# Dots that read normalised rows from PSUM, a weighted sum in one bank, and a fifth slot for v rows

## The reference, cut to what matters

```python
y, k_new, v_new, s_new = token_mixer(rmsnorm(h, norm1), ...)   # 8 attention heads and 4 recurrent heads
h = h + y
h = h + peer(rmsnorm(h, norm2), peer_w_q, peer_sub_keys, peer_u, peer_v)
out = rmsnorm(h, final_norm)

def peer(xn, ...):                       # per block of 128 tokens
    s = einsum('thcd,hcnd->thcn', qh, sub_keys)          # 8 heads, 2 halves, 128 keys
    ... top 16 of each half, of their 256 sums the top 16: 128 experts eidx a token
    act = gelu(einsum('td,thkd->thk', xb, u_tab[eidx]))  # u_tab: 16384 x 1024
    return einsum('thk,thkd->td', g * act, v_tab[eidx])  # v_tab: 16384 x 1024
```

## Time and profile before

| | |
|---|---|
| time, median of 3 runs | 4234.32 us (4230.32 to 4242.23) |
| span of the profiled execution, its own time | 4312.9 us |
| PE, DVE, POOL, ACT busy | 68%, 62%, 61%, 24% |
| moved by DMA | 1387.82 MB, mean 322 GB/s |
| gathers | 1152 of u, 1152 of v |

### The profile page before, as it was taken

One profiled execution on the slowest core, in us unless ns is written; L12 is line 12 of the kernel. 1 busy time (PEld: TensorE's weight loads), 2 busy tenths in 40 slices (PEclk: granted clock), 3 DMA queues, 4 the chain that ended last, 5 costly groups with the idle time before them and its releaser, 6 DMA issues. The chain is left out here.

```text
span 4312.9 us, 52328 instructions
## 1 busy us (share of the span) xinstructions
PE 2945.6 (68%) x18028; PEld 1552.0 (36%) x18028; DVE 2685.8 (62%) x7647; ACT 1054.1 (24%) x2841; POOL 2646.5 (61%) x2365
## 2 busy tenths in 40 slices
PE   7889997876577648774877487748784565333365
PEld 6745553533253325432443244325442231000011
DVE  2456667756875777567756876687658656644400
ACT  3312212222232222222222222222222211111121
POOL 1102434666776676577666765775567767777765
PEclk9999998777577758685778577857786666555556
DMA  7535898999999999898989998998898999999998
GB/s 202 179 127 184 283 334 287 334 367 347 331 344 366 332 332 335 312 357 323 333 312 364 342 335 308 364 339 319 307 358 309 377 361 359 329 371 364 364 368 316
DMA packets 568774, 1387.82 MB, mean 322 GB/s; under 512 B 57384, under 2 KB 252384, under 8 KB 568512
## 3 DMA queue, kind: packets, MB, share of 16 engines
q0 software_dynamic: 335024, 1215.35, 76.6%
q1 hardware_dynamic: 221264, 159.49, 11.9%
q10 hardware_dynamic: 12224, 9.63, 0.8%
HBM read 1353.19 MB, written 30.95 MB: 321 GB/s over the span
## 5 line engine op out<-in xcount | busy, mean ns | idle before, releaser
L1805 DVE CUSTOM_DVE_ANT_0 d_ub<-d_ub,d_xn 128x1024 f32<-128x1024 f32 x1152 | 1404.7, 1222 | 950.8 <-DMA d_ub<-in_peer_u_dram,d_eid 855.2
L1611 POOL DMA_INDIRECT d_ub<-in_peer_u_dram,d_eid x1152 | 1292.5, 1122 | 807.6 <-issue 313.5
L1628 POOL DMA_INDIRECT d_vb<-in_peer_v_dram,d_eidT x1088 | 1263.4, 1161 | 708.0 <-PE d_pY L1656 383.7
L1656 PE MATMUL d_pY<-d_vb,d_dg 128*32 128x256 f32 x8704 | 938.9, 522 | 1070.1 <-DMA d_vb<-in_peer_v_dram,d_eidT 949.0
L1656 PEld LDWEIGHTS d_pY<-d_vb,d_dg 128*32 128x32 f32 x8704 | 237.6, 127 | 1668.8 <-issue 1492.0
L1696 ACT ACTIVATE d_dg<-c_late_sb,d_wgtT 128x32 f32<-128x32 f32 x1152 | 342.4, 315 | 1399.9 <-PE d_pY L1656 1149.5
L680 PE MATMUL d_pY<-d_wq,d_vb 128*128 128x512 f32 (+3 forms) x1536 | 473.0, 461 | 14.2 <-DMA d_vb<-in_w_in_dram 7.7
L680 PEld LDWEIGHTS d_pY<-d_wq,d_vb 128*128 128x128 f32 x1536 | 269.4, 198 | 182.5 <-issue 115.5
L816 PE MATMUL d_pS<-t_shared 32*128 32x512 f32 (+3 forms) x384 | 194.9, 707 | 52.6 <-DMA t_shared<-scratch_kT 43.2
L827 PE MATMUL d_pS<-t_mdg,t_E 128*128 128x128 f32 x1152 | 219.0, 361 | 13.2 <-DVE t_mdg L1036 11.2
L827 PEld LDWEIGHTS d_pS<-t_mdg,t_E 128*128 128x128 f32 x1152 | 199.6, 266 | 73.5 <-issue 37.9
(11 more groups left out here) (257 smaller groups left out, 3521.1 us busy)
## 6 DMA issues: line engine op xcount, KB each, us to landing
d_vb<-in_w_in_dram SPq DMA_DIRECT2D x68, 512.0 KB
d_ub<-in_peer_u_dram,d_eid POOLq DMA_INDIRECT x1152
d_vb<-in_peer_v_dram,d_eidT POOLq DMA_INDIRECT x1088
r_side<-in_cache_k_dram SPq DMA_DIRECT2D x16, 1024.0 KB
r_side<-in_cache_v_dram SPq DMA_DIRECT2D x16, 1024.0 KB
d_wo<-in_w_out_dram SPq DMA_DIRECT2D x6, 2048.0 KB, 9.4
d_wo<-in_peer_w_q_dram SPq DMA_DIRECT2D x4, 2048.0 KB, 8.6
scratch_h<-t_shared SPq DMA_DIRECT2D x9, 512.0 KB
```

Of the source, the lines that this page charges most:

```text
L1611: pool.indirect_dma_start(out=ub[:, g % R, :], out_offset=None, in_=io["peer_u"][0], in_offset=off).then_inc(u_in[g % R], 16)
L1628: pool.indirect_dma_start(out=to, out_offset=None, in_=io["peer_v"][0], in_offset=off).then_inc(landed, 16)
L1656: m = nc.tensor.matmul(pY[q * QT:(q + 1) * QT, g // 2, (g % 2) * QD:(g % 2 + 1) * QD], dg[:, n % DG, :], rows[:, q * QD:(q + 1) * QD], sta ...
L1805: nc.vector.tensor_tensor_reduce(out=ub[:, g % R, :], in0=ub[:, g % R, :], in1=xn[:, i % 2, :], scale=1.0, scalar=0.0, op0=ALU.mult, op1=A ...
```

## The change

Five edits that depend on one another:

1. **Dots read PSUM.** The two banks that the projection used are now called `pX` and kept for one copy of the period's normalised rows. ACT makes the copy at the period's start (`copy_x`), after the last dot of the period before; the first dot waits for it. `d_xn` becomes a single buffer. Tile 0 of the order has no copy: its rows stand in the fifth v slot, and its 128 dots read both operands from SBUF as before.
2. **One bank for the weighted sum**, as two halves of 256 columns. DVE adds one group of 32 tokens at a time (256 columns), at k = 33, 65, 97 and at the start of the next period; PE's first product of each group waits for the addition of the group before. `load_xs` moves from k = 40 to k = 20.
3. **Three banks for the mixer.** `pT` is three blocks wide (TB = 3), `pO` is the rest of that bank. A tile of 4 blocks has two turns a head instead of one, of 7 or 8 blocks three instead of two. A head's first turn waits for the `output` of the head before. The search's products with the keys are made and copied in two halves.
4. **Five v slots** (RV = 5); in the last period nine with the u slots. The fifth is first used once period 0's dots are done.
5. The squares of the final norm write to `d_xn` in SBUF instead of PSUM.

The diff, cut to its core:

```diff
-    R = 4
+    R, RV = 4, 5
+    TB = 3
 def groups(t):
-        return -(-blocks(t) // 4)
+        return -(-blocks(t) // TB)
-        pY = ph.ps("d_pY", [P, 2, 512])
-        pS = ph.ps("d_pS", [P, 4, 512])
-        pT, pO = pS[:, 2, :], pS[:, 3, :]
+        pX = ph.ps("d_pX", [P, 2, 512])
+        pY = ph.ps("d_pY", [P, 2, QD])
+        pS = ph.ps("d_pS", [P, 3, 512])
+        pT, pO = pS[:, 2, 0:TB * P], pS[:, 2, TB * P:512]
...
             def turn(u, g):
                 if g == 0:
                     pe.wait_ge(mdg_done, 2 * (U + u + 1))
+                    if U + u:
+                        pe.wait_ge(o_done, U + u)
...
-            for g in range(2 * PH):
...
+            for c in range(2):
+                if c:
+                    yield local(i, R0 + 28.5)
+                    pe.wait_ge(r_done, 2 * i + 1)
+                for h in range(PH):
+                    m = nc.tensor.matmul(pS[:, h // 4, ...], mT[64 * c:64 * c + 64, h, :], keysT[64 * c:64 * c + 64, h, :], ...)
+                m.then_inc(r_psum, 1)
...
 # POOL, v gathers
+                            if n == RV - 1:
+                                pool.wait_ge(dot_done, NEXP)
-                            elif n >= R:
-                                pool.wait_ge(exp_used, n - (2 * R if n >= LAST + 2 * R else R) + 1)
+                            elif n >= RV:
+                                pool.wait_ge(exp_used, n - (RV + R if n >= LAST + RV + R else RV) + 1)
...
 # PE, weigh_rows
-                    if k == 0 and j:
-                        pe.wait_ge(h2_done, j)
+                    if k % QT == 0 and 4 * j + g:
+                        pe.wait_ge(h2_done, 4 * j + g)
...
+                def copy_x(i):
...
+                    act.wait_ge(xn_done, i + 1)
+                    act.wait_ge(dot_done, NEXP * i)
+                    nc.scalar.activation(xflat, xn[:], ACT.Copy).then_inc(x_copied, 1)
...
-                def residual(j):
-                    dve.wait_ge(exp_used, NEXP * (j + 1))
+                def residual(j, g):
+                    dve.wait_ge(exp_used, NEXP * j + QT * (g + 1))
                     dve.wait_ge(xs_in, 64 * (j + 1))
-                    nc.vector.tensor_tensor(xf, xf, yflat, ALU.add).then_inc(h2_done, 1)
+                    nc.vector.tensor_tensor(xs[:, g, :], xs[:, g, :], pY[:, g % 2, :], ALU.add).then_inc(h2_done, 1)
...
+                            if i and k == 0:
+                                dve.wait_ge(x_copied, i)
-                            nc.vector.tensor_tensor_reduce(out=ub[:, g % R, :], in0=ub[:, g % R, :], in1=xn[:, i % 2, :], scale=1.0,
+                            nc.vector.tensor_tensor_reduce(out=ub[:, g % R, :], in0=ub[:, g % R, :], in1=xflat if i else xn_of(0), scale=1.0,
```

More of the change, by code:

```diff
@@ L368, in layer @@
         u_in = [ph.sem(f"d_u_in{n}") for n in range(R)]
-        v_in = [ph.sem(f"d_v_in{n}") for n in range(2 * R)]
+        v_in = [ph.sem(f"d_v_in{n}") for n in range(RV + R)]
         ids_done, dot_done, gelu_done, wgt_done, wT_psum, wT_done = (ph.sem(n) for n in (
             "d_ids_done", "d_dot_done", "d_gelu_done", "d_wgt_done", "d_wT_psum", "d_wT_done"))
-        dg_done, exp_used = ph.sem("d_dg_done"), ph.sem("d_exp_used")
+        dg_done, exp_used, x_copied = ph.sem("d_dg_done"), ph.sem("d_exp_used"), ph.sem("d_x_copied")
         xs_in, h2_done, fsum, fq_psum, froot_done, y_done, y_stored = (ph.sem(n) for n in (
@@ L700, in near_block @@
                     pe.wait_ge(c_near_done, n - 1)
-                nc.tensor.matmul(pS[:, 2 + n % 2, :], flip, back[:, n].rearrange("p h k -> p (h k)"), start=True, stop=True).then_inc(c_near_psum, 1)
+                nc.tensor.matmul(aside_bank[n % 2], flip, back[:, n].rearrange("p h k -> p (h k)"), start=True, stop=True).then_inc(c_near_psum, 1)
             def keys(n):
@@ L733, in v_slot @@
             if n < LAST:
[L734 to L739, removed]
+                return vb[:, n % RV, :], v_in[n % RV], 16 * (n // RV + 1)
+            s = (n - LAST) % (RV + R)
+            turn = (n - LAST) // (RV + R) + 1
+            if s < RV:
+                slot = (LAST + s) % RV
+                return vb[:, slot, :], v_in[slot], 16 * ((LAST + s) // RV + turn)
+            return ub[:, s - RV, :], v_in[s], 16 * turn
         def local(i, at):
@@ L990, in mixer_scalar @@
             act.wait_ge(turned, 3 * i + 3)
-            nc.scalar.activation(mT[:].rearrange("p c n -> p (c n)"), pS[:, 2:4, :].rearrange("p a n -> p (a n)"),
+            nc.scalar.activation(mT[:].rearrange("p c n -> p (c n)"), pS[:, 0:2, :].rearrange("p a n -> p (a n)"),
                                  ACT.Copy).then_inc(turned_done, 1)
-            yield local(i, R0 + 29)
-            act.wait_ge(r_psum, i + 1)
-            nc.scalar.activation(S.rearrange("p g n -> p (g n)"), pSf, ACT.Copy).then_inc(r_done, 1)
+            for c in range(2):
+                yield local(i, R0 + 28 + 1.5 * c)
+                act.wait_ge(r_psum, 2 * i + c + 1)
+                nc.scalar.activation(S[:, c * PH:(c + 1) * PH, :].rearrange("p g n -> p (g n)"), pSf[:, 0:PH * PN],
+                                     ACT.Copy).then_inc(r_done, 1)
             yield local(i, R0 + 58)
@@ L1630, in _ @@
                     pool.wait_ge(u_in[n], 16 * (NT * NEXP // R))
-                for n in range(2 * R):
-                    _, landed, count = v_slot(NT * NEXP - 2 * R + n)
+                for n in range(RV + R):
+                    _, landed, count = v_slot(NT * NEXP - (RV + R) + n)
                     pool.wait_ge(landed, count)
@@ L1789, in finish @@
                     if i >= 2:
-                        residual(i - 2)
+                        residual(i - 2, 3)
                 for k in range(FIRST, 0):
@@ L1801, in _ @@
                             finish(i)
+                        if 1 <= i <= NT and k % QT == 1 and k > QT:
+                            residual(i - 1, k // QT - 1)
                         if i < NT:
```

97 lines of the change are left out of this document (54 added, 43 removed).

## The result

| | before | after | ratio, 95% interval |
|---|---|---|---|
| median us (range, runs) | 4232.32 (4211.72 to 4242.23, 4) | 4073.72 (4056.63 to 4077.94, 4) | 0.9626 (0.9593 to 0.9658) |

The change takes 3.7% off, 159 us. The forecast was 84 us, 4150, with a range from 4095 to 4235: the kernel is faster than the whole range. The profiled execution took 4077.21 us, as long as the timed ones, with a span of 4075.4.

What follows compares the result with a forecast made beforehand. DMA, kept from full by POOL's gather issue, was taken as the bound. Terms -98 (dots and slot), -2 (boundary), +8 and +6 (waits, coupling) gave -86 of 4312.9 us, scaled by 0.982 to -84: 4150 us, range 4095 to 4235.

Steps and rivals of the forecast that it cites:

- The mechanism of the lock: Six mixer periods: dots with two SBUF inputs lengthen POOL's gathers by 340 us; with one in PSUM most of it goes.
- Rival 2: Gather lengthening only coincides with dots and stays; only the fifth slot counts, gain 31 us, 4204 us; chance 0.08.
- the tenth I left: Gathers in the mixer periods: other instructions with two SBUF inputs keep perhaps a tenth of the 340 us of lengthening.
- Duration of a dot, boundary, tail: Dots stay at 1222 ns; at period boundaries the copy hides under a wait, 2 us gained; the tail gains nothing.
- Added waits and coupling: Extra PE waits in mixer and search cost 8 us; DVE and PE waiting on each other at 24 additions, 6 us.
- Rival 4: At the 24 grouped additions DVE stops for PE's lag, costing 144 us; slower, net +46, 4280 us; chance 0.10.
- So about 0.98 is what full looks like: DMA share of the eighth period taken as full; six mixer periods rise from 0.93 to 0.965, gaining 94 us.
- rival 1: Six mixer periods reach a DMA share of 0.98 and the coupling costs nothing: -141 us, 4096 us; chance 0.12.
- rival 3: DMA is full for the mixer periods at 0.93; POOL's freed 340 us become slot waits: +5 us, 4239; chance 0.09.
- 716 us of stalls and waits: POOL in the six mixer periods: 340 us of gather lengthening and 376 us of slot waits, about 300 going at once.
- the rest: POOL in the six mixer periods: 452 us, some 0.30 us ahead of each gather, unexplained by the profile; it stays.
- The slot is what lets the first edit count: With four v slots, a POOL that no longer stalls would only wait more for slots; a fifth covers most waits.

Runs made afterwards that it cites:

- e3: Changed kernel with four v slots instead of five (PSUM dots and the copy kept): 4123.63 us, ratio 0.9763 to the kernel before.
- e2: Changed kernel without PSUM dots and the fifth v slot (dots read SBUF, two buffers of normalised rows): 4214.7 us, ratio 0.9985 to the kernel before.
- e1: The kernel before, unchanged, profiled a second time: 4233.21 us, where its first profile took 4312.9.
- e4: The changed kernel, unchanged, timed and profiled again: 4070.85 us, ratio 0.9637 to the kernel before.
- e5: Changed kernel with five u and four v slots, first tile's expert output left wrong: 4259.32 us, ratio 0.9907 to the kernel before at 4300.55.
- e15: The changed kernel, unchanged, in a set at the lower transfer speed: 4275.45 us, ratio 0.9897 to the kernel before at 4323.4.

## Why the prediction was wrong

- **The mechanism of the lock: right.** Dots with two inputs in SBUF lengthen the gathers that start inside them; with one in PSUM they do not (632 gathers at 1.45 us, 506 at 0.95). Gathers measured 998 and 953 ns against 960 forecast, and e3 against e2, which differ in that alone and the copy it needs, is 91 us. The Trainium skill's inference ("SBUF — State Buffer", "Who interferes with whom"), that VectorE reading two SBUF inputs leaves descriptor generation alone, does not carry to these gathers: they were 1.45 us long beside such dots, 0.95 beside dots with one. Rival 2 is out. Which access of the gather is held up, that to its row numbers or another, no run tried. What lengthening stays is larger than the tenth I left: 770 x 61 + 768 x 16 ns = 59 us over the median of 937, most of it the expert search's two-input instructions.
- **Duration of a dot, boundary, tail: right.** 1216 ns; the dot waited 0.7 us in all for the copy; the tail is 170 us in e1 and after the change.
- **Added waits and coupling: too dear.** I took 8 + 6 us of cost less 2, together 12. e2, all of this with four slots, is 0.15% (10 us) faster than before, with an interval that reaches 0.11% (5 us) slower: at least 7 us of my cost were not there. PE's 45 us behind the additions is a little over my 40 and costs nothing that shows. Rival 4 is out.
- **"So about 0.98 is what full looks like": the step that failed**, with the sum that stands on it, 2606 x (1 - 0.93/0.965) = 94 us. It takes the DMA share for a fraction of a fixed capacity, so that a stretch shortens as its share rises. The runs show otherwise in two ways. First, 0.98 is not full: the eighth period, which moves the same bytes each time, ran at shares of 0.98, 1.02 and 1.03 and took 370, 341 and 331 us, and the middle one, the kernel before at the level of the timed runs, was bound by POOL. Second, time does not go with the share: from e1 to the changed kernel it went from 0.94 to 0.96, by my formula 2587 x (1 - 0.94/0.96) = 54 us (73 with the shares unrounded, 0.935 and 0.963), but the stretch shortened by 133. The same bytes passed at 359 instead of 341 GB/s. The forecast share of 0.96 to 0.97 came true, the length of 2510 us did not (2454).
- **The terms, on the medians of one set:** I took 98 us of gain for dots and slot together, where e3 and e4 show 91 + 53 = 144, and 12 us of cost, where e2 shows none. By stretches: the six periods -133 us, costs included, where I took -94 + 12 = -82; the seventh -14 where I took -4; the eighth -10 where I took 0. The six periods' 133 is also rival 1's bound; that is luck, for rival 1 reached it with a share of 0.98, and its time, 4096 us, is 22 over the measured one.
- **The trace came from another level than the timed runs.** I scaled by 0.982, as if profiling had stretched everything alike. At the trace's own level, the eighth period took 370 us (before), 367 (e5) and 370 (e15) whether POOL was busy 274 or 240 us, so "nothing" was right there; but the change as a whole gained 48 us where I took 86, and the share of the six periods rose to 0.94, not 0.965. There, rival 3's picture, freed time that turns into waits, is nearer to what happened than mine. My 84 us were met at neither level.
- **A link that I left out** is that POOL's waits grow when its stalls go. I counted 716 us of stalls and waits and let 300 go (the 452 us that I called the rest hold 35.5 us of waits for "remote" besides the gaps of 0.30 us); measured from e1 to e4, POOL's busy time fell by 298 us, its waits for slots rose by 260 and the unexplained "issue" gaps fell from 405 to 311 us, together 298 - 260 + 94 = 132; the stretch shortened by 130. That a gather which waits for a slot shows no gap of its own beside it is my reading of the last term.
- **"The slot is what lets the first edit count": wrong.** With four slots the dots alone give 91 of 154 us, and the slot 53 on top. What the slot would give without PSUM dots was not run.

## What to carry to other kernels

A busy share of DMA engines near 1 does not say that they are full: look at whether the engine that issues the transfers waits. In this kernel its issues stood back to back at a share of 1.02, it was the bound, and 10 us were to be had. And a rise of the share does not convert into time: 0.94 to 0.96 went with 5% off a stretch. Before adding up terms from a profile, hold its span against the timed runs; here 1.9% over all of them meant another level of transfer speed, on which the same change was worth a third, and not a factor to divide out. An instruction of VectorE that reads two operands from SBUF beside GpSimd's indirect DMAs is worth changing so that one comes from PSUM; here it was worth 91 us of 4215.

## What the runs showed of the hardware

- An indirect gather that starts inside a dot with two SBUF inputs takes 1.39 us in the earlier trace rows and 1.45 on average over 632 of them; inside a dot with one PSUM input it takes 0.93 in the row shown and 0.95 on average over 506. Inside an 864-column instruction with two SBUF inputs it is lengthened too, 1.82 us on average over 48.
- Whole sets of runs differ in transfer speed: the eighth period, gathers with dots and weighted sums alone, ran at 398 to 408 GB/s or at 367 to 369, and before took 4220 to 4232 or 4301 to 4323 us. The sets on chips 8 and 9 were the slow ones, those on 2, 5 and 10 the fast ones; what sets the level was not tried.
- The mean busy share of the DMA engines is not a measure of room: the same bytes took 370 us at a share of 0.98, 341 at 1.02 and 331 at 1.03.
- Three, four and five v slots with PSUM dots gave ratios of 1.0285 (lower level), 0.9763 and 0.9637 (higher). A slot more seems to change more when there are few; with the levels mixed, this is not shown.
